# Mixing by token tiles, statistics and router products between its blocks, norm weights behind the gather, nine weight units

## The reference

```python
merged = gate_s5 * y_s5 + gate_dn * y_dn
mix = merged @ w_mix_out                                   # 2048 x 2048
h = layer_norm(ALPHA * x + mix, ln1_g, ln1_b)              # ALPHA = 2 ** 0.25
logits = h @ w_router + b_router                           # 32 experts
top_val, top_idx = lax.top_k(logits, 4)
top_w = jax.nn.softmax(top_val)
# for every expert e, on the tokens that chose it:
gate = min(xb @ w_gate[e] + b_gate[e], 7)
up = clip(xb @ w_up[e] + b_up[e], -7, 7)
y = (gate * sigmoid(1.702 * gate) * (up + 1)) @ w_down[e] + b_down[e]
ffn = sum over the four experts of top_w * y
out = layer_norm(ALPHA * h + ffn, ln2_g, ln2_b)
```

## Time and profile before

| | us |
|---|---|
| median of 3 runs | 3056.47 (3056.23, 3056.47, 3060.41) |
| the profiled execution | 3061.29 |
| its span, first to last instruction | 3059.6 |
| TensorE busy (19635 matmul instructions) | 2913.5 (95%) |
| VectorE busy | 935.3 (31%) |
| ScalarE busy | 471.6 (15%) |
| DMA: 653.96 MB | mean 214 GB/s |

### The profile page before, as it was taken

How to read it: one execution, slowest core, us unless ns; L and a number is a source line. 1 busy time by engine, 2 the same in 40 slices (tenths; PEclk the granted TensorE clock), 3 DMA queues, 4 the chain that set the end, 5 groups by cost and what they waited for, 6 DMA issues and landing times.

```text
span 3059.6 us, 47372 instructions
## 1 busy us (share of the span) xinstructions
PE 2913.5 (95%) x19635; PEld 2099.8 (69%) x19635; DVE 935.3 (31%) x2066; ACT 471.6 (15%) x625; POOL 100.8 (3%) x179
## 2 busy tenths in 40 slices
PE   8999999999999999999999999849999999999995
PEld 7888888888788888888888888734443444334341
DVE  2432433423423237777700000140121112112115
ACT  2221231231221122110010000001111111111101
POOL 2010010001000000000000000000000000000000
PEclk9999999999999999999999999959999999999998
DMA  7233243342253433334445456417999999999993
GB/s 202 84 111 111 84 138 96 99 137 82 88 144 98 146 111 111 111 115 134 138 138 165 139 163 247 164 64 327 421 422 422 422 422 422 422 422 422 422 421 162
DMA packets 319130, 653.96 MB, mean 214 GB/s; under 512 B 38816, under 2 KB 268320, under 8 KB 268512
## 3 DMA queue, kind: packets, MB, share of 16 engines
q1 hardware_dynamic: 318976, 651.59, 57.7%
HBM read 649.47 MB, written 2.10 MB: 213 GB/s over the span
## 4 chain that ended last, share of the span: by engine, by line
PE 55%; issue 16%; DVE 13%; DMA 9%; DVEq 3%; ACT 1%; POOLq 1%; POOL 1%; SPq 1%; ACTq 0%
PE bank L895 11%; PE bank L589 10%; DMA arena<-in_w_up_dram 8%; PE bank L1058 7%; PE bank L1023 7%; DVE arena L1626 4%; PE bank L1012 4%; PE bank L925 4%; PE bank L1074 4%; DVE arena L1630 3%; DVE arena L1628 3%; PE bank L663 1%; PE bank L681 1%; PE bank L674 1%; PE bank L1034 1%
## 5 line engine op out<-in xcount | busy, mean ns | idle before, releaser
L589 PE MATMUL bank<-arena 128*128 128x256 f32 x4096 | 934.2, 383 | 0.0
L589 PEld LDWEIGHTS bank<-arena 128*128 128x128 f32 x4096 | 765.0, 190 | 112.4 <-issue 8.0
L1023 PE MATMUL bank<-arena 128*64 128x512 f32 x2048 | 446.1, 594 | 8.4 <-DMA arena<-in_w_up_dram 8.4
L1023 PEld LDWEIGHTS bank<-arena 128*64 128x64 f32 x2048 | 144.4, 137 | 308.1 <-issue 286.5
L895 PE MATMUL bank<-arena 128*128 128x256 f32 x1536 | 331.8, 379 | 0.0
L895 PEld LDWEIGHTS bank<-arena 128*128 128x128 f32 x1536 | 291.8, 190 | 39.9 <-issue 0.3
L1058 PE MATMUL bank<-arena 128*64 128x512 f32 x1024 | 223.3, 594 | 7.7 <-ACT masks L1335 7.7
L834 PE MATMUL bank<-arena 128*128 128x256 f32 x1024 | 223.5, 380 | 0.0
L834 PEld LDWEIGHTS bank<-arena 128*128 128x128 f32 x1024 | 194.0, 190 | 27.3 <-issue 0.9
L1058 PEld LDWEIGHTS bank<-arena 128*64 128x64 f32 x1024 | 72.1, 137 | 148.5 <-issue 137.0
L1864 DVE TENSOR_SCALAR arena<-bank 128x512 f32<-128x512 f32 x16 | 11.1, 692 | 479.3 <-PE bank L1023 479.3
(11 more groups left out here) (295 smaller groups left out, 2005.0 us busy)
## 6 DMA issues: line engine op xcount, KB each, us to landing
arena<-in_w_in_dram SPq DMA_DIRECT2D x72, 2048.0 KB, 8.7
arena<-in_w_gate_dram SPq DMA_DIRECT2D x64, 2048.0 KB, 16.9
arena<-in_w_up_dram SPq DMA_DIRECT2D x64, 2048.0 KB, 16.0
arena<-in_w_down_dram SPq DMA_DIRECT2D x64, 2048.0 KB, 20.6
arena<-in_w_dn_out_dram SPq DMA_DIRECT2D x16, 2048.0 KB, 8.4
arena<-in_w_glu_b_dram SPq DMA_DIRECT2D x8, 2048.0 KB, 8.2
arena<-in_w_glu_a_dram SPq DMA_DIRECT2D x8, 2048.0 KB, 8.2
...
```

The costliest lines, as they stand in the source:

```text
L589: last = mm(ps[bank][:, ct * T:ct * T + T], ring[:, buf, k, ct * P:ct * P + P], rhs[:, k, :], start=k == 0, stop=k == KD - 1)
L1023: last = mm(ps[bank][CAP * o:CAP * o + CAP, :], xg[:, 4 * q + k, CAP * o:CAP * o + CAP], w[:, o, k], start=False, stop=q == 3 and k == 3, ...
```

## The change

- **Mixing by token tiles.** Sixteen blocks `mix(n)`: tile 0 for eight columns, then tile 1, of 256 columns each. All eight weight tiles stay in SBUF (`mixw`); six are loaded during GLU, two as GLU ends. The barrier goes: `mix(0)` waits for the merges of GLU but the last, and before its 15th product for the last. x comes in two halves.
- **Between the blocks** TensorE transposes the block before (`turn_acc`), ScalarE copies it (`copy_turn`), TensorE multiplies it with the router's weights (`router_part`). VectorE gathers statistics per block. The logits are built from the products of what is not yet normalised: the router's weights are multiplied by `ln1_g`, and mean, root and the two column sums are put in afterwards (`prepare_router`, `take_sums`, `choose`). These weights and norm vectors are loaded in GLU, two of them element by element (`gkp`, `bkp`).
- **Selection** by two top-8 instructions per tile. Tile 0 is normalised, selected and placed while tile 1 is mixed.
- **Norm weights behind the gather.** `h1` is only standardised, by ScalarE (`standardise`); `ln1_g` and `ln1_b` are applied by ScalarE in `sgather` and `turn_h1`, four passes over 128 columns instead of one copy of 512; `acc` gets ALPHA times the normed value (`residual`).
- **Bias of the down product** goes into the first pair's scatter (`bias_part`, eight products of 32 rows); TensorE transposes the weights in pair 0 (`turn_wt`).
- **Nine weight units**: three more buffers (`extra`), used once, for units 6, 7 and 8 of pair 0. Units 0 to 5 are loaded as the blocks of tile 1 free the mixing weights. The pair 1 is written out ahead of the loop.
- **Final norm**: statistics between the last additions, two passes instead of four, root by one function whose table is loaded ahead, output in four halves.

Cut to its core:

```diff
+        mixw = [at(off, KD, SC) for off in (OT, OT + 4096, 12288, SH + 8192, SH + 12288, SH + 16384, 0, 4096)]
+        piece = (at(TM + 512, 2, P), at(SH + 20480, 2, P))
...
+        unit = [at(off, 2, 4 * F_E) for off in (OT, OT + 4096, 12288, SH + 8192, SH + 12288, SH + 16384)]
+        extra = [at(off, 2, 4 * F_E) for off in (8192, SH + 20480, XT)]
...
+            def load_mix(r):
+                sp.dma_start(mixw[r], tile_rows(w_mix[:, SC * r:SC * r + SC])).then_inc(
+                    mix_loaded if r < 6 else late_mix_loaded[r - 6], 16)
+            def load_router():
+                sp.wait_ge(y_taken, NCH)
+                sp.dma_start(gw, w_router.rearrange("(k p) e -> p k e", p=P)).then_inc(router_loaded, 16)
+                sp.dma_start(gkp, ln1_g.rearrange("(k p) -> p k", p=P), allow_slow_non_contiguous=True).then_inc(router_loaded, 16)
+                sp.dma_start(bkp, ln1_b.rearrange("(k p) -> p k", p=P), allow_slow_non_contiguous=True).then_inc(router_loaded, 16)
+                sp.dma_start(gqk, ln1_g.rearrange("(p k) -> p k", k=KD)).then_inc(router_loaded, 16)
+                sp.dma_start(bqk, ln1_b.rearrange("(p k) -> p k", k=KD)).then_inc(router_loaded, 16)
+                sp.dma_start(brt, b_router.partition_broadcast(P)).then_inc(router_loaded, 16)
+            for c in range(1, COLS):
                 load_glu(c)
-            for r, bank in enumerate((2, 1, 0)):
-                load_slot(r, tile_rows(w_mix[:, SC * r:SC * r + SC]), bank, MIX_USE[bank])
-            sp.wait_ge(phase_done[2], 4)
-            sp.dma_start(acc, x[0].rearrange("(m p) d -> p m d", p=P)).then_inc(x_loaded, 16)
+                if c == 1:
+                    load_router()
+                if c <= 6:
+                    load_mix(c - 1)
+            sp.wait_ge(bank_ready[2], GS5_USE + COLS)
+            load_mix(6)
+            sp.wait_ge(bank_ready[1], GLU_USE + COLS)
+            load_mix(7)
+            sp.wait_ge(bank_ready[0], GLU_USE + COLS)
+            xv = x[0].rearrange("(m p) d -> p m d", p=P)
+            for m in range(MT):
+                sp.dma_start(acc[:, m], xv[:, m]).then_inc(x_loaded[m], 16)
             sp.dma_start(lnrow[:, 0], ln1_g.partition_broadcast(P)).then_inc(ln_loaded, 16)
...
             def reload_unit(j, i):

-                sp.wait_ge(unit_read[j % UNITS], 2 * i + j // UNITS)
+                sp.wait_ge(unit_read[j % UNITS], 2 * i + j // UNITS - (1 if j % UNITS < 3 else 0))
                 sp.sem_inc(load_free, 1)
...
-            load_unit(0, 0)
-            load_unit(1, 0)
-            for r in range(3, 8):
-                load_slot(r % RING, tile_rows(w_mix[:, SC * r:SC * r + SC]), r % 3, MIX_USE[r % 3] + r // 3)
-            for j in range(2, UNITS - 1):
+            load_extra(UNITS)
+            for j in range(UNITS):
+                sp.wait_ge(mix_ready, COLS + j + 1)
                 load_unit(j, 0)
+            sp.wait_ge(mix_ready, MIXES)
+            for c, b in enumerate((b_gate, b_up)):
+                sp.dma_start(bias_gu[0:N_E, c], b).then_inc(brow_loaded, 16)
+            for n in range(4):
+                sp.dma_start(bdn4[N_E * n:N_E * n + N_E], b_down[:, F_E * n:F_E * n + F_E]).then_inc(bdn_loaded, 16)
+            sp.wait_ge(log_done, MIXES)
+            load_extra(UNITS + 1)
+            sp.wait_ge(resid_done, MT)
...
+            def mix(n):
+                m, r = divmod(n, COLS)
+                bank = 3 + n % 3
+                if n == 0:
+                    pe.wait_ge(glu_used, COLS)
+                if n == 0:
+                    pe.wait_ge(mix_loaded, 96)
+                if n in (6, 7):
+                    pe.wait_ge(late_mix_loaded[n - 6], 16)
+                if n >= 3:
+                    pe.wait_ge(acc_ready, n - 2)
+                for k in range(KD):
+                    if n == 0 and k == KD - 2:
+                        pe.wait_ge(glu_used, COLS + 1)
+                    last = mm(ps[bank][:, 0:SC], mg[:, k, m * P:m * P + P], mixw[r][:, k, :],
+                              start=k == 0, stop=k == KD - 1)
+                last.then_inc(mix_ready, 1)
+            def turn_acc(n):
+                m, r = divmod(n, COLS)
+                pe.wait_ge(acc_ready, n + 1)
+                if n >= 2:
+                    pe.wait_ge(tr_taken, n - 1)
+                for j in range(2):
+                    last = tr(ps[6 + n % 2][:, j * P:j * P + P], acc[:, m, SC * r + j * P:SC * r + j * P + P], ident[:, :])
+                last.then_inc(tr_ready, 1)
+            def router_part(n):
+                m, r = divmod(n, COLS)
+                pe.wait_ge(tr_taken, n + 1)
+                for j in range(2):
+                    last = mm(ps[2 - 2 * m][:, 0:N_E], piece[n % 2][:, j], gw[:, 2 * r + j, :],
+                              start=r == 0 and j == 0, stop=r == COLS - 1 and j == 1)
+                last.then_inc(log_done, 1)
+            for n in range(MIXES):
+                mix(n)
+                if n == 1:
+                    pe.wait_ge(gw_ready, 1)
+                    mm(ps[1][:, 0:N_E], ones[:, :], cand[:, 0], start=True, stop=True)
+                    mm(ps[1][:, N_E:2 * N_E], ones[:, :], cand[:, 1], start=True, stop=True).then_inc(sums_ready, 1)
+                if n >= 1:
+                    turn_acc(n - 1)
+                if n >= 2:
+                    router_part(n - 2)
+                if n == 13:
+                    pe.wait_ge(sel_ready, 1)
...
+                    mm(ps[1][:, 0:N_E], ones[:, :], sel[:, 0], start=True, stop=False).then_inc(pos_ready, 1)
+            router_part(MIXES - 2)
+            turn_acc(MIXES - 1)
+            router_part(MIXES - 1)
+            pe.wait_ge(sel_ready, 2)
+            mm(ps[1][:, 0:N_E], upper, sel[:, 1], start=False, stop=True).then_inc(pos_ready, 1)
+            mm(ps[2][:, N_E:2 * N_E], ones[:, :], sel[:, 1], start=False, stop=True).then_inc(pos_ready, 1)
...
+            def turn_wt():
+                pe.wait_ge(wt_ready, 1)
...
+            def bias_part(bank, n, last):
+                rows = slice(N_E * (n % 4), N_E * (n % 4) + N_E)
+                return mm(ps[bank][:, :], wtT4[rows, (n // 4) * P:(n // 4) * P + P], bdn4[rows, :],
+                          start=True, stop=last, skip_group_check=True)
...
+            def await_unit(j, i):
+                if isinstance(i, int) and i == 0 and UNITS <= j < UNITS + 3:
+                    pe.wait_ge(extra_loaded[j - UNITS], 16)
+                    return extra[j - UNITS], extra_read
+                b = j % UNITS
...
+                biased = isinstance(i, int) and i == 0
+                if biased:
+                    pe.wait_ge(wtt_taken, 1)
...
-                              ysb[:, (n % 4) * 512:(n % 4) * 512 + 512], start=True, stop=True)
+                    bank = (2, 3, 0, 1)[n % 4]
+                    if biased:
...
                 sup(i)
+                if first:
...
+            pe.wait_ge(xhat_done, MT)
+            gather(0)
             pe.wait_ge(flag_ready, 1)
             over = pe.value_load(flag[0:1, 0:1], min_val=0, max_val=1)
             with pe.If(over < 1):
-                gather(0)
                 sparse(0, first=True)
-                with pe.Fori(1, PAIRS - 1) as i:
+                sparse(1)
+                with pe.Fori(2, PAIRS - 1) as i:
                     sparse(i)
...
+            def copy_turn(n):
+                act.wait_ge(tr_ready, n + 1)
+                if n >= 2:
+                    act.wait_ge(log_done, n - 1)
+                nc.scalar.copy(piece[n % 2], ps[6 + n % 2][:, 0:SC].rearrange("p (j t) -> p j t", j=2)).then_inc(tr_taken, 1)
...
+            def standardise(m):
+                root(m, m)
+                act.wait_ge(nmr_ready, m + 1)
+                A(h1[:, m].rearrange("p k q -> p q k"), acc[:, m].rearrange("p (q k) -> p q k", k=KD), ACT.Identity,
+                  scale=lnv(m, RSTD), bias=lnv(m, NMR))
+                act.drain()
+                act.sem_inc(xhat_done, 1)
...
+            for n in range(COLS - 1):
+                copy_turn(n)
+            standardise(0)
+            for n in range(COLS - 1, MIXES):
+                copy_turn(n)
+            standardise(1)
+            act.wait_ge(sel_ready, 2)
             for m in range(MT):
-                act.wait_ge(ln_step, m + 1)
-                v = stats[:, 50:51]
-                A(v, v, ACT.Ln, bias=eps_ln)
-                act.drain()
-                A(v, v, ACT.Exp, scale=-0.5)
...
             def sgather(i):
...
                     act.wait_ge(xg_done, 4 * i + b + 1)
-                    nc.scalar.copy(xg[:, 4 * b:4 * b + 4, :], ps[4 + b][:, :].rearrange("p (k t) -> p k t", k=4)).then_inc(xg_taken, 1)
+                    for j in range(4):
+                        k = 4 * b + j
+                        last = A(xg[:, k, :], ps[4 + b][:, P * j:P * j + P], ACT.Identity,
+                                 scale=gqk[:, k:k + 1], bias=bqk[:, k:k + 1])
+                    last.then_inc(xg_taken, 1)
...
```

(80 more changed lines are left out.)

427 lines of the change are left out of this document (202 added, 225 removed).

## The result

The changed kernel takes **2984.97 us** (median of four runs, 2983.63 to 2987.02), the kernel before 3056.39 beside it: ratio 0.9756, 95% interval 0.9744 to 0.9768. 2979.0 was forecast, with a range of 2968 to 2996. The profiled execution has a span of 2984.3 us; before it was 3059.6. So 75.3 us went from the span, where the steps of the prediction sum to 79.0. By the medians it is 71.4: the profiled execution of the kernel before lies 4.8 us above its median, that of the changed kernel 1.1.

The account below looks back on a forecast made before the run. Bounds: a 95.3 us dent of serial steps after mixing; in the expert stage the DMA engines, by 0.8 us a pair. Terms summed to -79.0: 2982.3 from the profiled execution, 2977.5 from the median; forecast 2979, bounds 2968 to 2992, (b) to 2996.

Parts of the forecast that it names:

- GLU's end to mixing: Handoff from TensorE's last GLU product to the first mixing product: last merge hidden, barrier wait gone, -2.0 us.
- mixing: Mixing stage: same products, plus transposes, router parts and sums between them on TensorE, +10.5 us (up to +15).
- mixing to first expert product: After mixing's last block: a chain of small steps, gather and last copy take 18.2 us instead of 95.3, -77.1 us.
- expert stage: Expert pairs: bias products delay buffers, DMA engines stand still, then bind again; +4.3 us, bounds -3 to +8.
- tail: Last pair's scatter to the end: statistics between additions, fewer norm passes, roots hidden; 26.9 instead of 41.6 us, -14.7.
- Handoff and router loads: GLU into mixing: last merge hidden, -2.0 us; router loads of some 15 us covered by 19 us to spare, cost 0.
- rival (d): Before the selection: late statistics or router loads leave TensorE standing, some 60 of 77 us stay: 3040; chance 0.02.
- (b): Mixing: handshakes between engines cost a 1 us stall each, 16 us more, or permuted ScalarE pass doubles: 2995; chance 0.12.
- (c): Mixing: interludes halve the granted clock throughout, its 110.8 us take twice as long: +32, 3089; chance 0.02.
- The nine units: Expert stage weight loads: three extra buffers serve once, giving the DMA engines 4.5 us of lead instead of 14.9.
- rival (a): Expert stage: nine units keep the DMA engines ahead, TensorE alone binds, 3 us less instead of 4.3 more: 2972; chance 0.14.

Follow-up runs that it names:

- e11: Changed kernel with transposes, their copies, router products and tile 0's selection moved after the last mixing block: 2986.24 us, ratio 0.9766 to the kernel before.
- e5: Changed kernel plus 17 unread identity products filling TensorE's waits between mixing and the first gate: 2981.18 us, ratio 0.9750 to the kernel before.
- e1: Changed kernel without the eight bias products of the down projection in pair 1 (b_down left out): 2973.72 us, ratio 0.9726 to the kernel before.
- e2: Changed kernel with six weight buffers as before, the three extra ones taken away: 2984.17 us, ratio 0.9756 to the kernel before.
- e9: Changed kernel with nine buffers as one ring throughout and pairs written out without loops on any engine: 2978.68 us, ratio 0.9737 to the kernel before.

## Why the prediction was right, and where its terms were off

| step | forecast | measured |
|---|---|---|
| GLU's end to mixing | -2.0 | -2.2 |
| mixing | +10.5 | +9.9 |
| mixing to first expert product | -77.1 | -78.3 |
| expert stage | +4.3 | +9.8 |
| tail | -14.7 | -13.7 |
| ahead of mixing | 0 | -0.8 |
| sum | -79.0 | -75.3 |

The forecast of 2979 stood between 2982.3, which the steps give on the profiled execution, and 2977.5 on the median. Against the changed kernel's profiled execution (2986.08) the steps are 3.8 us short; no term was off by more than its own bounds except the expert stage, forecast as +4.3 with +8 at most.

GLU's end to mixing: 0.17 us of overlap (1866.47 against 1866.30) stand where 1.99 us of waiting stood.

**Handoff and router loads** held. TensorE never waits in GLU, so rival (d), loads that come late, fell; the two loads of single elements kept SP's queue for 6.38 and 1.37 us (two times 3.27 was reckoned from the earlier trace rows), all six for 12.2 (1576.90 to 1589.09), and no GLU product waited.

**Mixing** held. The interlude takes 0.58 us, where 0.24 + 0.47 was reckoned: the router's four instructions take 0.36 to the next start. e11, which leaves only the two products of the column sums in mixing, has it 9.5 us shorter. Rivals (b) and (c) fell: 120.64 us without a wait at a granted clock of 1.00.

**Mixing to experts**: the mechanism was right, with single terms off on both sides. The gather starts at 6.6 (7.2), takes 8.75 (9.9), and its last block costs 1.59 (1.15). The 8.75 are this execution's: the nine other traces without e5's products have 8.93 to 10.01, so that the 9.9 was a fair price. The last block: four ScalarE passes of 128 columns take 1.50 us and not the 1.07 drawn from the copies of the earlier trace rows. Intercept and slope of plain copies don't give the price of a pass that reads scale and bias per partition.

**The expert stage is the term that was mis-sized**, by 5.5 us. The chain was as forecast: a gap of the DMA engines in pair 1, waits for w_up from pair 6 on, 0.8 us a pair. Counted from the first gate product (2005.79), the gap lies from 104.6 to 113.8 us, 9.2 long, where 101.3 to 109.0 was forecast. The prediction's own terms give 99.9 for its start (20.4 and sixteen units of 4.97) and not 101.3; its total does not hang on this, for it goes by the gap's end. Two terms of it were too small. Eight bias products were put at 0.88 us, from the scatter's products alone; they took 1.05 each and made each neighbour take 1.05 instead of 0.887, so that pair 1 grew by 10.0 us (e1) instead of 7.1. And the low clock, which the prediction let end with the gather, came back in the first gate: 1.7 us in this execution, none in others (e5). These are 4.6 of the 5.5, and the gap's end is 4.8 late; the rest stays open.

**The nine units.** The prediction set their lead at 4.5 us instead of 14.9, which was right in what it said (rival (a) fell: the waits came), but it did not say that the gap in pair 1 takes even that. e2 shows it: six units give the same time. Used throughout, the same three buffers are worth 8.5 us (e9).

**The tail** was 1.0 us longer. Additions and statistics took 1.39 us a block, where 1.38 was reckoned (rows at 2957.58 and 2958.97):

```profile
2957.58 0.69 DVE L2069 TENSOR_TENSOR arena<-arena,bank 128x512 f32<-128x512 f32 x1 [15.76 <-PE bank L1165]
...
2958.97 0.67 DVE L2069 TENSOR_TENSOR arena<-arena,bank 128x512 f32<-128x512 f32 x1
...
2971.40 2.35 DVE L2090 SCALAR_TENSOR_TENSOR arena<-arena,small 128x2048 f32<-128x2048 f32 x1 [0.78 <-ACTq L1402]
...
2978.65 2.48 DVE L2095 SCALAR_TENSOR_TENSOR arena<-arena,small 128x1024 f32<-128x1024 f32 x2
```

The root of tile 1 is not hidden: VectorE waits 0.78 us for ScalarE. That is most of the difference.
